# First expert's row numbers straight from the slot table, its second weight piece behind its gathers, and ScalarE and VectorE steps reordered in a routed-expert kernel

## The reference

```python
xp = xp + mix @ w_out[l]
h_all = rms(x, norm2_g)
logits = h @ w_router + b_router
top_val, top_idx = lax.top_k(logits, 4)
gate = softmax(top_val)
# per expert e, for the rows routed to it:
up = xblk @ w_up[e] + b_up[e]
x_glu = minimum(up[..., :1024], 7.0)
x_lin = clip(up[..., 1024:], -7.0, 7.0)
act = x_glu * sigmoid(1.702 * x_glu) * (x_lin + 1.0)
y = (act @ w_down[e] + b_down[e]) * gate
# y is added to the rows' residuals
```

## Time and profile before

| | |
|---|---|
| median of 3 runs | 2725.3 us (2721.98 to 2728.66) |
| the profiled execution's own time | 2730.6 us |
| its span, first to last instruction | 2728.9 us |
| busy: TensorE, VectorE, ScalarE, POOL | 93%, 33%, 24%, 18% |
| DMA | 533.64 MB, mean 196 GB/s |
| mean granted TensorE clock | 0.964 |

### The profile page before, as it was taken

One profiled execution on the slowest core, in us unless ns is written; L12 is line 12 of the kernel. 1 busy time (PEld: TensorE's weight loads), 2 busy tenths in 40 slices (PEclk: granted clock), 3 DMA queues, 4 the chain that ended last, 5 costly groups with the idle time before them and its releaser, 6 DMA issues.

```text
span 2728.9 us, 44704 instructions
## 1 busy us (share of the span) xinstructions
PE 2550.6 (93%) x18242; PEld 2127.6 (78%) x18242; DVE 906.3 (33%) x2491; ACT 646.6 (24%) x1644; POOL 489.9 (18%) x476
## 2 busy tenths in 40 slices
PE   7999979989989779869999999999999999999994
PEld 3555546446656544569999999999999999999994
DVE  1223244237666433424222232222323232222321
ACT  1212122137656312301111111111111111111111
POOL 0000032010000201311232222131323231221211
PEclk9999989989999879979999999999999999999997
DMA  5000075031000442477778778888899999989994
GB/s 201 13 24 22 14 176 113 1 112 73 1 1 1 129 142 85 142 239 247 244 254 277 258 268 296 284 277 295 295 313 307 334 315 320 326 306 324 317 330 146
DMA packets 283537, 533.64 MB, mean 196 GB/s; under 512 B 52754, under 2 KB 96114, under 8 KB 283122
## 3 DMA queue, kind: packets, MB, share of 16 engines
q1 hardware_dynamic: 235298, 474.35, 49.0%
q0 software_dynamic: 33504, 46.98, 8.1%
q10 hardware_dynamic: 14528, 9.41, 1.3%
HBM read 492.21 MB, written 42.96 MB: 196 GB/s over the span
## 4 chain that ended last, share of the span: by engine, by line
PE 60%; DMA 1%; DVE 1%; ACT 0%; issue 0%; POOL 0%; SPq 0%; POOLq 0%; DVEq 0%; ACTq 0%
PE eo L2189 37%; PE eo L2200 18%; PE eo L2068 5%; DMA w_up<-summed_rows 1%; PE erp L2104 1%; DMA slot_tokens_gates<-token_gate_s,dest_s 0%; DMA slot_rows<-slot_tokens_gates 0%; ACT hT_e L2227 0%; DVE window_rows L2334 0%; DMA summed_rows<-window_rows,row_index_cur 0%; SPq L2007 0%; POOL summed_rows L2023 0%; POOL x_rows L2017 0%; DMA x_rows<-h_rows,row_index_cur 0%; PE rankp L2136 0%
## 5 line engine op out<-in xcount | busy, mean ns | idle before, releaser
L2189 PE MATMUL eo<-rg_oret,w_up 128*128 128x128 f32 (+19 forms) x4096 | 507.8, 286 | 8.7 <-DVE rg_oret L2469 8.7
L2189 PEld LDWEIGHTS eo<-rg_oret,w_up 128*128 128x128 f32 x4096 | 504.7, 192 | 9.0 <-DVE rg_oret L2469 9.0
L2200 PE MATMUL eo<-rg_oret,mixT 128*128 128x128 f32 (+19 forms) x4096 | 507.8, 286 | 0.0
L2189 PE MATMUL eo<-rg_oret,cache_rows 128*128 128x128 f32 (+19 forms) x4096 | 505.2, 285 | 0.0
L2200 PEld LDWEIGHTS eo<-rg_oret,mixT 128*128 128x128 f32 x4096 | 503.6, 191 | 1.1
L2189 PEld LDWEIGHTS eo<-rg_oret,cache_rows 128*128 128x128 f32 x4096 | 502.1, 191 | 0.0
L2023 POOL DMA_INDIRECT summed_rows<-window_rows,row_index_cur x153 | 241.2, 1576 | 1082.3 <-ACT window_rows L2272 1045.5
L2488 DVE TENSOR_SCALAR window_rows<-eo,b_up_cur 128x128 f32<-128x128 f32 (+19 forms) x256 | 93.5, 365 | 1004.6 <-PE eo L2189 1004.6
L358 PE MATMUL zp<-w_in,xnT 128*128 128x512 f32 (+2 forms) x800 | 305.4, 538 | 1.4 <-DVE xnT L576 1.4
L2283 ACT ACTIVATE window_rows<-window_rows 128x128 f32<-128x128 f32 (+19 forms) x256 | 82.5, 322 | 853.0 <-DVE window_rows L2488 853.0
L358 PEld LDWEIGHTS zp<-w_in,xnT 128*128 128x128 f32 x800 | 145.9, 193 | 139.2 <-issue 122.4
(11 more groups left out here) (455 smaller groups left out, 2044.2 us busy)
## 6 DMA issues: line engine op xcount, KB each, us to landing
w_up<-in_w_up SPq DMA_DIRECT2D x64, 2048.0 KB
cache_rows<-in_w_up SPq DMA_DIRECT2D x64, 2048.0 KB, 13.7
mixT<-in_w_down SPq DMA_DIRECT2D x64, 2048.0 KB, 10.9
w_in<-in_w_in SPq DMA_DIRECT2D x3, 2048.0 KB, 12.5
x<-in_x_prompt SPq DMA_DIRECT2D x8, 512.0 KB, 4.0
window_rows<-in_x_prompt SPq DMA_DIRECT2D x8, 512.0 KB, 3.6
summed_rows<-window_rows SPq DMA_DIRECT2D x8, 512.0 KB, 2.7
h_rows<-h SPq DMA_DIRECT2D x8, 512.0 KB, 3.6
```

Of the source, the lines that this page charges most:

```text
L2189: mm = nc.tensor.matmul(up[c % 2][:, h, :N], U[c // 4][:, h, kk, w0:w0 + P], hT[:, kk, :N], start=(kk == 0), stop=(kk == KC - 1))
L2200: mm = nc.tensor.matmul(dn[d % 2][:, :N], Dn[:, kk // 4, kk % 4, d * P:d * P + P], aT[:, kk, :N], start=(kk == 0), stop=(kk == KC - 1))
```

## The change

- **Row numbers.** A new helper `load_first_slots` reads the token numbers of the first expert's first 128 slots from DRAM as single elements, 128 of them for each of the four quarters, into a small tile `slots0`; SP issues two of the four loads and ScalarE's queue two, both behind a wait for all scatters. VectorE makes the first expert's row numbers from it in one instruction. The way over the whole table stays for the second and later experts.
- **SP's list.** The sample's `h` stores come first, on a semaphore of their own; then the wait for the scatters, the new loads, the table read, the sample's residual stores. The first expert's piece 1 is asked for behind its gathers, ahead of the down weights. POOL waits for the residual stores only before its first add.
- **ScalarE's list.** In each pass `evict(t-1)` stands ahead of `square(t, 0)`; in the last pass the root's table is loaded ahead of `evict(7)`, which stands before `square(7, 1)`.
- **TensorE's list.** Each half of the router waits for its own half of `hT_e`; `out(1, 0)` moves ahead of the gain columns; two of the sample's chunks move behind the last tile's ranks.
- **VectorE's list.** The norm of the last tile moves behind the sample's copy of `hT_e`, the norm of the sample rows behind their destinations. The slots are reduced straight into integers, without the copy.
- **Homes.** `ln` and `sg` move to `x2[1]`, `gm` to `h[1]`.

```diff
--- before.py
+++ after.py
@@ -1818,11 +1818,12 @@
         v8, i8, f8 = sb("top8", [P, 8]), sb("top8_at", [P, 8], mybir.dt.uint32), sb("top4_at", [P, TOPK])
         gd, gs = sb("gate_exp", [P, 2, TOPK]), sb("gate_sum", [P, 2])
         pair = sb("token_gate", [P, PT, TOPK, 2])
-        slot, hd, df = sb("slot", [P, NE]), sb("slot_hot", [P, TOPK, NE]), sb("destf", [P, TOPK])
+        slot, hd = sb("slot", [P, NE]), sb("slot_hot", [P, TOPK, NE])
         dest, pair_s, dest_s = sb("dest", [P, PT, TOPK], I32), sb("token_gate_s", [P, 2]), sb("dest_s", [P, 1], I32)
         mine, bigger, hot32, number = sb("own_key", [NE, 2]), sb("bigger", [NE, NE]), sb("place_hot", [NE, NE]), sb("expert_number", [NE, P])
         far, firstf, first = sb("first_far_behind", [P, NE]), sb("first_f", [P, 2]), sb("first_expert", [P, 1], I32)
-        spare = sb("table_trigger", [P, 2])
+        spare = sb("table_trigger", [P, 3])
+        slots0 = sb("first_slots", [P, 4])
 
         U = [k.early[:], nat.rearrange("p (h c n) -> p h c n", h=2, c=KC)]
         Dn = mix[:, 0:8 * D].rearrange("p (q c n) -> p q c n", q=2, c=4)
@@ -1831,8 +1832,8 @@
         idx_n, gate_n, bu_n = sb("row_index_cur", [P, 4, 8], I32), sb("gates_cur", [P, 2, 8]), sb("b_up_cur", [P, 4, 16])
         xg = sb("x_rows", [P, NG, 256])
         ysb = natw[:, 0:NG * 256].rearrange("p (a x) -> p a x", a=NG)
-        wide = lambda n: natw[:, NG * 256 + 2 * CAP * n:NG * 256 + 2 * CAP * (n + 1)].rearrange("p (b n) -> p b n", b=2)
-        gl, ln, sg, gm = (wide(n) for n in range(4))
+        wide = lambda ap: ap.rearrange("p (b n) -> p b n", b=2)
+        gl, ln, sg, gm = (wide(home[:, 0:2 * CAP]) for home in (natw[:, NG * 256:2 * D], x2[1], x2[1][:, 2 * CAP:], h[1]))
         old = k.rg_oret[:]
         hT, yT = (old[:, n * KC * PAD:(n + 1) * KC * PAD].rearrange("p (c n) -> p c n", c=KC) for n in range(2))
         aT = old[:, 2 * KC * PAD:2 * KC * PAD + KC * CAP].rearrange("p (c n) -> p c n", c=KC)
@@ -1866,6 +1867,7 @@
         s_b, s_bt, s_bc, s_n = sem("bias_loaded"), sem("bias_transposed"), sem("bias_ready"), sem("order_ready")
         s_u = [sem(f"up_piece_loaded{q}") for q in range(2)]
         s_wd = [sem(f"down_piece_loaded{q}") for q in range(2)]
+        s_i0, s_hs = sem("first_slots_loaded"), sem("sample_h_stored")
         s_il, s_io, s_is, s_ix = sem("slots_loaded"), sem("block_slots_loaded"), sem("slots_spread"), sem("row_index_ready")
         s_tu, s_rp, s_gc, s_gn = sem("slots_turned"), sem("slots_replicated"), sem("gate_columns_ready"), sem("gates_cur_ready")
         s_z, s_ov = sem("buffers_zeroed"), sem("overflow_listed")
@@ -1922,8 +1924,13 @@
         def overflow_expert(eng, b):
             return eng.value_load(obe[0:1, bass.ds(b, 1)], min_val=0, max_val=NE - 1)
 
+        def load_first_slots(eng, e, quads):
+            src = k.slot_dram[bass.ds(e, 1), 0:P, 0:1].rearrange("o (a j) w -> (o j) a w", j=32)
+            with nc.allow_non_contiguous_dma(reason="one list, small"):
+                for q in quads:
+                    eng.dma_start(slots0[32 * q:32 * q + 32, :].unsqueeze(2), src).then_inc(s_i0, 16)
+
         def load_slots(eng, h):
-            eng.wait_ge(s_sc, 16 * (PT * TOPK + 1))
             eng.dma_start(got[:, h], k.slot_dram[16 * h:16 * h + 16, 0:256, :].rearrange("e (a i) w -> e a (i w)", i=32)).then_inc(s_il, 16)
 
         @block.sync
@@ -1968,16 +1975,17 @@
                 sp.wait_ge(s_h, t + 1)
                 sp.dma_start(k.acc_dram[t * P:t * P + P, :], x2[t % 2]).then_inc(s_st[t % 2], 16)
                 sp.dma_start(k.h_dram[t * P:t * P + P, :], h[t % 2][:]).then_inc(s_st[t % 2], 16)
-            sp.wait_ge(s_o, 2 * NT)
-            load_up(e0, 1)
             sp.wait_ge(s_h, NT)
             for b in range(4):
-                c0 = slice(256 * b, 256 * b + 256)
-                sp.dma_start(k.h_dram[S:T, c0], h[0][32 * b:32 * b + 32, 0:256]).then_inc(s_st[0], 16)
-                sp.dma_start(k.acc_dram[S:T, c0], x2[0][32 * b:32 * b + 32, 0:256]).then_inc(s_st[0], 16)
+                sp.dma_start(k.h_dram[S:T, 256 * b:256 * b + 256], h[0][32 * b:32 * b + 32, 0:256]).then_inc(s_hs, 16)
+            sp.wait_ge(s_sc, 16 * (PT * TOPK + 1))
+            load_first_slots(sp, e0, (0, 1))
             load_slots(sp, 0)
+            for b in range(4):
+                sp.dma_start(k.acc_dram[S:T, 256 * b:256 * b + 256], x2[0][32 * b:32 * b + 32, 0:256]).then_inc(s_st[0], 16)
             for a in range(groups_of[0]):
                 sp.wait_ge(s_xg[a], 16)
+            load_up(e0, 1)
             load_down(e0)
             sp.wait_ge(s_n, 1)
             for n in range(1, NE):
@@ -2033,14 +2041,16 @@
             nc.gpsimd.indirect_dma_start(out=slots, out_offset=at_rows(dest_s[:]), in_=pair_s[:], in_offset=None).then_inc(s_sc, 16)
 
             placed = lambda n: (lambda a: idx_n[:, n % 4, a:a + 1])
-            pool.wait_ge(s_st[0], 32 * 4 + 128)
+            pool.wait_ge(s_st[0], 32 * 4)
             pool.wait_ge(s_st[1], 32 * 4)
+            pool.wait_ge(s_hs, 64)
             pool.wait_ge(s_ix, 1)
             gather(0, placed(0), groups_of[0])
             nc.gpsimd.memset(yT, 0.0)
             nc.gpsimd.memset(got_o[:], 0.0).then_inc(s_z, 1)
             pool.wait_ge(s_ix, 2)
             gather(1, placed(1), groups_of[1])
+            pool.wait_ge(s_st[0], 32 * 4 + 64)
             for n in range(NE):
                 add_rows(n, placed(n), groups_of[n])
                 if n + 2 < NE:
@@ -2096,10 +2106,10 @@
                 nc.tensor.transpose(tp[y][:, 0, :], x2[0][:, y * P:y * P + P], ident).then_inc(s_t, 1)
 
             def router(t):
-                pe.wait_ge(s_te, 2 * t + 2)
                 if t >= 1:
                     pe.wait_ge(s_l, t)
                 for y in range(2):
+                    pe.wait_ge(s_te, 2 * t + 1 + y)
                     for b in range(4):
                         mm = nc.tensor.matmul(rp[:, 0:NE], hT_e[:, 4 * y + b, :], wr[:, 2 * b + y, :],
                                               start=(y == 0 and b == 0), stop=(y == 1 and b == 3))
@@ -2131,13 +2141,15 @@
             for m in range(6):
                 mm = nc.tensor.transpose(tp[m // 4][:, m % 4, :], braw[:, m, :], ident)
             mm.then_inc(s_bt, 1)
+            out(1, 0)
             pe.wait_ge(s_one, 2)
             for c in range(KC):
                 mm = nc.tensor.matmul(rk[:, 256 + c:257 + c], gain[0:1, c * P:c * P + P], ones[0:1, 0:1], start=True, stop=True)
             mm.then_inc(s_gT, 1)
             for t in range(1, PT):
-                out(t, 0)
-                if t == 1:
+                if t >= 2:
+                    out(t, 0)
+                else:
                     pe.wait_ge(s_bc, 1)
                     pe.wait_ge(s_wr, 1)
                 turn(t - 1)
@@ -2155,10 +2167,10 @@
             out_sample(0, range(0, 4))
             router(PT - 1)
             out_sample(0, range(4, KC))
-            out_sample(1, range(0, 6))
+            out_sample(1, range(0, 4))
             ranks(PT - 1)
             turn_sample(0)
-            out_sample(1, range(6, KC))
+            out_sample(1, range(4, KC))
             router_sample(0)
             turn_sample(1)
             pe.wait_ge(s_ss, 2 * PT + 1)
@@ -2237,13 +2249,15 @@
             act.dma_start(braw[:, 4:6, :], bdn).then_inc(s_b, 16)
             act.wait_ge(s_one, 1)
             for t in range(PT):
+                if t >= 1:
+                    evict(t - 1)
                 square(t, 0)
                 if t >= 1:
-                    evict(t - 1)
                     gates(t - 1)
+                if t == PT - 1:
+                    nc.scalar.activation(spare[:, 2:3], eps[:], ACT.Sqrt)
+                    evict(t)
                 square(t, 1)
-                if t == PT - 1:
-                    evict(t)
                 root(t)
             gates(PT - 1)
             nc.scalar.activation(spare[:, 0:1], eps[:], ACT.Sqrt)
@@ -2262,8 +2276,10 @@
                 last = nc.scalar.activation(pair_s[SR * j:SR * j + SR, 1:2], gd[:SR, PT % 2, j:j + 1], ACT.Copy,
                                             scale=gs[:SR, PT % 2:PT % 2 + 1])
             last.then_inc(s_pd, 1)
+            act.wait_ge(s_sc, 16 * (PT * TOPK + 1))
+            load_first_slots(act, ordered_expert(act, 0), (2, 3))
             load_slots(act, 1)
-            act.wait_ge(s_ix, 1)
+            act.wait_ge(s_ix, 2)
             nc.scalar.copy(gate, spread[:, 8 * NE:16 * NE]).then_inc(s_gc, 1)
 
             def scaled(n, gate, ng):
@@ -2377,14 +2393,15 @@
                 dve.wait_ge(s_rk, t + 1)
                 link(V.tensor_tensor(slot[:R], rk[:R, 0:NE], ebase[:R], ALU.add))
                 link(V.tensor_tensor(hd[:R], hot[:R, t % 2], slot[:R].unsqueeze(1).broadcast_to([R, TOPK, NE]), ALU.mult))
-                link(V.tensor_reduce(df[:R], hd[:R], AX.X, ALU.add))
                 if t < PT:
-                    V.tensor_copy(dest[:, t, :], df[:])
```

(21 more changed lines are left out.)

## The result

| | before | after |
|---|---|---|
| median of the timed runs | 2726.98 us (4 runs, 2721.98 to 2732.74) | 2701.70 us (4 runs, 2699.48 to 2705.78) |
| ratio of the times after to before, with its 95% interval | | 0.991 [0.9888, 0.9931] |
| profiled execution: its own time, span | 2730.6, 2728.9 us | 2705.78, 2704.1 us |

The change saves 25.3 us of median. The forecast was 30.1, to 2695.2: the result lies inside the range of 2690 to 2709 and 6.5 above its middle. Against the profiled execution's own time the forecast was 2700.5.

The account below looks back on a forecast made before the run. The experts keep TensorE busy, so only their start can move. Savings of 7.3 (gaps), 6.7 (clock), 1.9 (pass 1) and 14.2 (behind the loop) sum to 30.1, taking 2725.3 to 2695.2 us; range 2690 to 2709.

Parts of the forecast that it names:

- Gaps of the passes 2 to 7: Token-tile loop: TensorE's idle time ahead of the router, waiting for ScalarE's copies, goes; 7.3 us saved.
- Clock in these passes: Passes 2 to 7: four slow sets of 32 projections return to 13.83 us; 6.7 us saved, bounds 0 and 6.7.
- Rival (a): Loop: the clock falls go on and only the gaps go; 21.5 us saved, 2704 us; chance 0.15.
- Pass 1: Loop's first pass: projection ahead of gain turns starts the router 3.4 us earlier, a clock fall may follow; 1.9 saved.
- Sample rows: Between loop and last scatter: the moved norms and the slots' reductions start the last scatter 0.6 us earlier.
- Scatter: Last scatter before the first expert: without the second 4 MB it lands after 2.3 us, not 8.42; 6.1 saved.
- Rival (b): Before the first expert: scatter and small loads stay slow without load, 6 us lost; 2701 us; chance 0.10.
- Row numbers: From scatter landing to first gather: single-element loads take 4.7 us instead of 12.2; 7.5 saved, bounds 5 and 8.
- Second 4 MB: First expert's second piece, asked for behind the gathers: lands 14.8 us behind the first matmul, 2.3 to spare, cost 0.
- rival (c): First expert: the second piece, sharing the queue with the down weights, comes late, a 7.4 us stall; 2703; chance 0.07.
- Moved activation tiles: Experts: new homes of the four activation tiles, same shapes, cost 0.
- rival (e): Experts: moved activation tiles slow operations, paid 32 times; 1.2 us an expert makes it slower, 2734 us; chance 0.03.

Follow-up runs that it names:

- square_first: The kernel after with ScalarE's first square ahead of its copies again, the router's two halves kept: 2709.33 us in one run.
- router_whole: The kernel after with the router waiting for both halves again, the copies still ahead of the square: 2704.86 us in one run.
- piece1_late_only: The kernel before with one edit, the first expert's second 4 MB asked for behind its gathers: 2721.12 us (10 runs), ratio 0.9981 to before.
- gain_first: The kernel after with the projection out(1, 0) behind the gain turns again: 2695.36 us in one run.
- pass1_covered: The kernel after with the projection half out(1, 1) moved between the first transposes and the first router: 2697.65 us (4 runs), ratio 0.9895 to before.
- whole_table: The kernel after with the first expert's row numbers taken over the whole table again, second piece still late: 2701.8 us (4 runs), ratio 0.9912 to before.
- after_again: The kernel after, unchanged, run and profiled again: 2701.36 us (5 runs), ratio 0.9906 to before.
- loop_only: The kernel before with the loop's part of the change alone: 2715.35 us (8 runs), ratio 0.9968 to before.

## Why the forecast was right, and what it mis-sized

The forecast held: its case, its range, and nearly its sum. Held against the execution it was made from, A to C is 30.1 shorter in after, the number forecast. That this fits to the decimal is luck: by the same two executions the passes 2 to 7 gave 0.6 more than booked, the sample rows 0.4 and the row numbers 0.7 more, pass 1 gave 1.2 less and the scatter 0.5 less. Step by step:

- **Gaps of the passes 2 to 7** (7.3): gone, right. It takes both edits (4.9 are left in square_first, 2.5 in router_whole).
- **Clock in these passes** (6.7): right, 13.8 in each. Rival (a), falls that go on, is out for the passes 2 to 6 and right for the first. The router and the transposes ahead of it are a little shorter too (router 1.91 for 1.97): these passes gave 14.6 in all where 14.0 was forecast (7.3 and 6.7).
- **Pass 1** (1.9 saved, bounds 0 and 3.4): this term was mis-sized. The steps were placed rightly: the router starts 12.35 behind A, where the forecast's times have it 13.0 behind, and 16.38 in its execution, so 4.0 were won ahead of it. But the fall behind the long light stretch, which the forecast named and priced at 1.7, took 1.1 on the router (3.06) and 2.2 on the projections (16.07 for 13.83), 3.3 in all. From A to the end of the 32 projections behind the first router, less their 13.8, before has 18.4 in the execution of the forecast and in piece1_late_only, 16.7 and 16.8 in the two later profiles; the six profiles with the new order of projection and gain turns and all of the loop's other edits have 17.2 to 18.1 (after 17.7 and 17.4). So 0.7 was saved by the forecast's own execution, 0.7 to 0.9 lost by the two later ones, and over all ten profiles it comes to nothing (17.6 in the mean on both sides). gain_first and pass1_covered take the light stretch apart, and in both the router and the projections behind it are not slow; gain_first, with this edit taken back, has 15.4 in its one profile. The bound of 0 had no reason either, for nothing excluded a loss.
- **Sample rows** (0.6): from the end of the loop's last projection to the last scatter it was 15.9 before (1143.12 to 1158.98) and is 14.9 after (1133.73 to 1148.58), 1.0 saved. Right.
- **Scatter** (6.1, from 8.42 to 2.3): 2.85, so 5.6 against that execution; 4.3 against the later ones (7.0 to 2.8). Rival (b), small transfers slow without load, is out.
- **Row numbers** (7.5, from 12.2 to 4.7): 4.0, so 8.2 against that execution and 7.0 against the later ones (10.9 to 11.0 there). The new way was sized well; whole_table shows that only 2.8 of it is the new way's.
- **Second 4 MB** (cost 0, landing 14.8 behind the first matmul): it lands 16.8 behind (16.6 in after_again), where TensorE comes to it. The margin of 2.3 was eaten up and 0.2 paid; in the profiles with the piece at this place the wait was 0 to 1.0 us (1.0 in router_whole, none in whole_table, gain_first and pass1_covered). The landing was taken from a place where 4 MB flew beside six gathers with nothing asked for behind them; here the same six gathers are beside it, and the down weights are asked for 1.2 us behind it on the same queue. That this sharing, the mechanism of rival (c), made the 2 us is argued and not shown; its price of 7.4 was not paid.
- **Moved activation tiles** (0, rival (e)): C to end 1542.2, 1541.6 and 1541.5 before, 1541.5 and 1541.9 after; out. (Its price of 1.2 us an expert leaves out the 0.06 that the forecast allowed as free; with it 1.26 is needed.)

Two of the forecast's own signs of being wrong showed up in small: a set of 32 projections above 15.5 us (16.07, in pass 1), and a wait for the second piece in the first expert (0.2, at the place and by the cause named). Neither touched the case that was forecast.

Why then 6.5 above the point? 4.8 are the saving (25.3 for 30.1) and 1.7 the median of before, which came out at 2727.0 where 2725.3 had been shown. 2695.2 was the median less 30.1. The execution that gave the durations was 5.3 above that median, and the forecast left open where those 5.3 lay. At least 4.3 of them lay in the terms: its A to C is that much longer than in two further executions, at the first projection (1.7 with the gain turns, slow in two profiles of four), the scatter and the read, just the rows whose shortening was booked. So this is the second thing mis-sized: the sum fits its own execution and must not be taken off the median in full. The timed interval of the ratio (18.8 to 30.5 us) would not exclude a saving of 30.1; that it is nearer 26 rests on the stages of two later profiles of before and two of after.

What stays open: why the clock falls in the passes 2 and 4 to 6 of before and never in 3, at the same gap; why the first projection of before took 8.77 in two profiles and 10.05 in two; and why the timed runs of loop_only show less than its stage.

## What to carry to other kernels

A large transfer that is not needed yet should be asked for behind the small ones that are on the path, even if its margin goes to nothing: place it by the landing it needs, then try one place earlier and one later. Before a saving is taken off a median, see whether the profiled execution was slow in the very rows that are booked, with a second profile of the same kernel. Where TensorE has several short dependent steps in a row, put a dense block between them rather than ahead of them.

## What was not expected of the hardware

- A 4 MB load in flight made each small transfer measured beside it two to three times slower: the last scatter 6.7 to 8.4 us against 2.5 to 3.1 without it, the table read 6.6 to 7.9 against 2.3 to 3.3, the 512 single elements 8.2 from issue to index against 2.8, a gather 6.2 against 2.8.
- The 512 single elements cost little: 0.81 us on SP and 0.86 on ACT to issue, 2.8 from the first issue to the index. The Trainium skill ("DMA: Bandwidth & Descriptors", Rules for kernel authors) advises against a strided last dim, as each element becomes a descriptor; at this size the measured rows say that it is cheaper by 2.8 us than the contiguous read of the whole table with the steps behind it (whole_table).
- TensorE's slow passes repeat from execution to execution, pass by pass (four profiles with before's loop), and one came behind a gap of 0.45 us.
